# Ten raw buffers during expert 0, and a first gather in full single precision

## What is computed

```
def swiglu(h, w_gu, w_down):
    gu = h @ w_gu
    return (jax.nn.silu(gu[..., :FF_DIM]) * gu[..., FF_DIM:]) @ w_down

def moe_swiglu(h, w_router, w_gu, w_down):
    logits = (h @ w_router).astype(jnp.float32)
    top_vals, top_idx = lax.top_k(logits, TOP_K)
    gates = jax.nn.softmax(top_vals, axis=-1)
    comb = jnp.sum(jax.nn.one_hot(top_idx, N_EXPERTS, dtype=jnp.float32) * gates[..., None],
                   axis=-2).astype(h.dtype)
    y = jnp.zeros_like(h)
    for e in range(N_EXPERTS):
        y = y + comb[..., e:e + 1] * swiglu(h, w_gu[e], w_down[e])
    return y
```

## Time and profile before

| | us |
|---|---|
| runs | 1605.94, 1602.95, 1606.61 |
| median | 1605.94 |
| the profiled execution, its own time | 1605.62 |
| span of the profiled execution | 1603.5 |
| TensorE busy in it | 1525.8 (95%) |
| VectorE busy | 1244.3 (78%) |
| ScalarE busy | 1017.5 (63%) |
| GpSimd busy | 144.9 (9%) |
| DMA, mean rate | 284 GB/s |

### The profile page before, as it was taken

How to read it: one execution, slowest core, us unless ns; L and a number is a source line. 1 busy time by engine, 2 the same in 40 slices (tenths; PEclk the granted TensorE clock), 3 DMA queues, 4 the chain that set the end, 5 groups by cost and what they waited for, 6 DMA issues and landing times.

```text
span 1603.5 us, 21400 instructions
## 1 busy us (share of the span) xinstructions
PE 1525.8 (95%) x7237; PEld 1252.7 (78%) x7238; DVE 1244.3 (78%) x1094; ACT 1017.5 (63%) x922; POOL 144.9 (9%) x111
## 2 busy tenths in 40 slices
PE   8999999999989988889999999999999999999997
PEld 6888777888879866667887887788788878887875
DVE  6744655544459978898888989898989898889898
ACT  5344444344345756687776777777777777787785
POOL 0000000000000002803102202000130022000000
PEclk9999999999999989999999999999999999999999
DMA  9653455555553035999998999999999999999994
GB/s 343 228 188 129 150 191 184 184 183 186 197 169 106 27 132 173 396 397 364 396 383 313 384 375 331 365 356 375 340 389 359 370 343 388 357 371 340 372 369 176
DMA packets 197770, 456.10 MB, mean 284 GB/s; under 512 B 9076, under 2 KB 17852, under 8 KB 197695
## 3 DMA queue, kind: packets, MB, share of 16 engines
q1 hardware_dynamic: 193340, 444.84, 76.6%
q0 software_dynamic: 1728, 5.27, 0.9%
q10 hardware_dynamic: 2626, 4.93, 0.9%
HBM read 452.90 MB, written 2.11 MB: 284 GB/s over the span
## 4 chain that ended last, share of the span: by engine, by line
PE 75%; DVE 13%; DMA 4%; issue 4%; ACT 4%; DVEq 0%; ACTq 0%; POOL 0%; POOLq 0%; SPq 0%
PE bank L1869 17%; PE bank L1862 11%; PE bank L1863 11%; PE bank L1951 6%; DVE wlo L1095 5%; PE bank L1860 5%; PE bank L1940 4%; DMA raw<-in_moe_w_gu 4%; DVE y L1366 4%; PE bank L2104 3%; ACT whi L591 3%; PE bank L1892 3%; PE bank L1899 2%; PE bank L1893 2%; PE bank L1942 2%
## 5 line engine op out<-in xcount | busy, mean ns | idle before, releaser
L1095 DVE TENSOR_TENSOR wlo<-raw,whi 128x2048 fp32r<-128x2048 f32 x422 | 957.0, 2290 | 256.0 <-ACT whi L591 254.4
L591 ACT ACTIVATE whi<-raw 128x2048 fp32r<-128x2048 f32 x422 | 800.5, 1918 | 405.3 <-PE bank L1869 260.6
L1869 PE MATMUL bank<-wlo,xx 128*128 128x512 f32 x1200 | 328.6, 396 | 23.0 <-DVE wlo L1095 22.1
L1869 PEld LDWEIGHTS bank<-wlo,xx 128*128 128x128 f32 x1200 | 222.6, 189 | 86.3 <-DVE wlo L1095 41.6
L1862 PE MATMUL bank<-whi,xx 128*128 128x512 f32 x640 | 251.8, 393 | 1.5 <-DVE xx L1121 0.6
L1863 PE MATMUL bank<-whi,xx 128*128 128x512 f32 x640 | 249.7, 390 | 0.0
L1860 PE MATMUL bank<-whi,xx 128*128 128x512 f32 x560 | 157.3, 403 | 5.8 <-ACT whi L591 5.8
L1862 PEld LDWEIGHTS bank<-whi,xx 128*128 128x128 f32 x640 | 120.6, 188 | 27.2 <-issue 1.0
L1863 PEld LDWEIGHTS bank<-whi,xx 128*128 128x128 f32 x640 | 120.6, 188 | 24.5
L1860 PEld LDWEIGHTS bank<-whi,xx 128*128 128x128 f32 x560 | 104.3, 190 | 32.9 <-issue 12.0
L1951 PE MATMUL bank<-wlo,hT 128*128 128x512 f32 x392 | 107.5, 396 | 1.2 <-DVE wlo L1095 1.2
(11 more groups left out here) (326 smaller groups left out, 1818.0 us busy)
## 6 DMA issues: line engine op xcount, KB each, us to landing
raw<-in_moe_w_gu SPq DMA_DIRECT2D x224, 1024.0 KB, 7.5
raw<-in_moe_w_down SPq DMA_DIRECT2D x112, 1024.0 KB, 7.9
raw<-in_ffn_w_gu SPq DMA_DIRECT2D x28, 1024.0 KB, 5.0
raw<-in_ret_w_in SPq DMA_DIRECT2D x24, 1024.0 KB, 7.5
raw<-in_ffn_w_down SPq DMA_DIRECT2D x14, 1024.0 KB, 4.9
raw<-in_ret_w_out SPq DMA_DIRECT2D x8, 1024.0 KB, 4.9
raw<-in_conv_w_pw SPq DMA_DIRECT2D x16, 512.0 KB, 4.5
raw<-in_conv_w_pw SPq DMA_DIRECT2D x4, 1024.0 KB, 5.3
```

Source lines behind the costliest of these rows:

```text
L591: nc.scalar.activation(whi[base % SPLIT][:, :], raw[base % RAW][:, :], ACT.Copy).then_inc(hi_done, 1)
L1095: nc.vector.tensor_tensor(wlo[base % SPLIT][:, :], raw[base % RAW][:, :], whi[base % SPLIT][:, :].bitcast(f32), ALU.subtract).then_inc(lo_ ...
L1869: last = nc.tensor.matmul(dst[:, :], both, wl, start=False, stop=kc == DC - 1)
```

## The change

Expert 0's blocks use a ring of ten buffers: the six of `raw` and four `spare` ones that lie in the region behind `conv_at`, where `yh`, `sq`, `yl` and `hT32` are. `home` gives the buffer of a block. Blocks 0 to 5 lie in `raw`, 6 to 9 in the spares, 10 to 35 go round the ten, and 36 to 41 are in `raw` again, so that experts 1 and on find the ring of six. Of the first round, block 6 waits for the counter `lnb_ps` (end of the convolution's norm), block 8 for lo of block 0, block 9 for `lgT_ps` (router products done); from block 10 each waits for the block that had its buffer before.

Since the buffer of a block now is not a plain function of a loop variable, expert 0's steps are written out on SP, ScalarE and VectorE, in all variants of need, and the loop over e starts at 1 there. TensorE's loops stay. The `If(e > 0)` of ScalarE and VectorE become a choice at build time.

The gather of expert 0 multiplies z, scaled in place by ScalarE, with `onehot`, both as plain float32: 16 products, in place of 32 with fp32r operands and of the two that clear. `zh` and `zl` are gone, and so are VectorE's two instructions for `zl`. The copy of z to `z_rows` is issued before the gather's results are read. The side expert's two fetches go to place 2, behind its `build_onehot`, since their buffers are those of a spare; the side expert's own `build_onehot` stays at place 1.

```diff
+        spare = [at("spare0", [P, BLK], f32, m_at), at("spare1", [P, BLK], f32, conv_at + 8192),
+                 at("spare2", [P, BLK], f32, m_at + 8192), at("spare3", [P, BLK], f32, conv_at + 16384)]
+        ring = raw + spare
...
+        FIRST_RING = [(B_MOE + i) % RAW for i in range(RAW)] + [RAW + i for i in range(len(spare))]
+
+        def home(block, six=0):
+            turn_of = block - B_MOE
+            if not isinstance(six, int) or not 0 <= turn_of < MOE_BLOCKS:
+                return block % RAW
+            return FIRST_RING[turn_of % (len(ring) if turn_of < MOE_BLOCKS - RAW else MOE_BLOCKS - RAW)]
...
             def load(base, src, six=0):
-
-                if base >= RAW:
-                    sp.wait_ge(lo_done, base - RAW + 1 + 6 * six)
-                dst = raw[base % RAW][:, :].rearrange("p (c n) -> p c n", c=src.shape[1])
-                sp.dma_start(dst, src).then_inc(arrived[base % RAW], 16)
+                base, six = absolute(base, six)
+                place = home(base, six)
+                before = user_before(base) if isinstance(six, int) and base < B_MOE + MOE_BLOCKS else base - RAW
+                if before >= 0:
+                    sp.wait_ge(lo_done, before + 1 + 6 * six)
+                elif place == RAW:
+                    sp.wait_ge(lnb_ps, 1)
+                elif place == RAW + 2:
+                    sp.wait_ge(lo_done, B_MOE + 1)
+                elif place == RAW + 3:
+                    sp.wait_ge(lgT_ps, TILES)
+                dst = ring[place][:, :].rearrange("p (c n) -> p c n", c=src.shape[1])
+                sp.dma_start(dst, src).then_inc(landed_in[place], 16)
...
-                if place == 1:
+                if place == 2:
                     for t in range(2):
                         fetch(2 + t, SIDE, t).then_inc(side_rows_in, 16)
+                if place == 1:
                     build_onehot(side_onehot, SIDE).then_inc(side_onehot_done, 1)
...
-                nc.scalar.activation(zh[:, t, :], z[:, t, :], ACT.Copy, scale=rstd[:, t:t + 1]).then_inc(zh_done, 1)
-            nc.scalar.activation(identr[:, :], ident, ACT.Copy).then_inc(zh_done, 1)
+                nc.scalar.activation(z[:, t, :], z[:, t, :], ACT.Copy, scale=rstd[:, t:t + 1]).then_inc(zn_done, 1)
             hi(B_MOE + 2)
+            nc.scalar.activation(identr[:, :], ident, ACT.Copy).then_inc(identr_done, 1)
             act.wait_ge(lg_max, 1)
             nc.scalar.activation(rk[:, 0, :, :], rk[:, 7, :, :], ACT.Exp).then_inc(ex_done, 1)
             nc.scalar.activation(warm[:, 0:1], smallT[:, 0:1], ACT.Silu)
+            act.wait_ge(zn_done, 2)
+            for t in range(TILES):
+                act.dma_start(z_rows[t * P:(t + 1) * P, :], z[:, t, :]).then_inc(z_stored, 16)
...
-                with dve.Fori(0, STEPS - 1) as i:
+
+                def step(i):
                     lo(B_MOE + 6, six + i)
                     hidT_lo(done + 1 + i)
                     lo(B_MOE + 7, six + i)
...
+                if later:
+                    with dve.Fori(0, STEPS - 1) as i:
+                        step(i)
+                else:
+                    for i in range(STEPS - 1):
+                        step(i)
...
                     for t in range(TILES):
-                        where = rows_of[:, t, tile * P:(tile + 1) * P]
-                        nc.tensor.matmul(dst, zh[:, t, c * P:(c + 1) * P], where, start=t == 0, stop=False)
-                        last = nc.tensor.matmul(dst, zl[:, t, c * P:(c + 1) * P], where, start=False, stop=t == TILES - 1)
+                        last = nc.tensor.matmul(dst, z[:, t, c * P:(c + 1) * P],
+                                                onehot[:, t, tile * P:(tile + 1) * P].bitcast(f32),
+                                                start=t == 0, stop=t == TILES - 1)
...
-            pe.wait_ge(zh_done, 3)
-            first_gather()
+            pe.wait_ge(zn_done, TILES)
+            pe.wait_ge(onehot0_done, 1)
+            gather(0, gather_ps).then_inc(gather_ps, 1)
+            pe.wait_ge(identr_done, 1)
```

129 lines of the change are left out of this document (76 added, 53 removed).

## The result

| | us |
|---|---|
| before, five runs beside the changed kernel | 1606.29 median (1602.95 to 1606.61) |
| changed kernel, five runs | 1595.50 median (1595.16 to 1598.05) |
| ratio | 0.9946, 95% interval 0.9934 to 0.9958 |
| profiled execution of the changed kernel | 1595.50, span 1593.7 |
| forecast | 1593.4 (1589.6 to 1597.5) |

The change gains 10.8 us, against 12.2 (the sum) forecast. A second series gave 1598.32 against 1605.38 (ratio 0.9958, 0.9944 to 0.9972): there it gains 7.1. So the size was missed by 1.4 to 5.1 us, and it was missed where the prediction had put a 5% rival. The first series lies inside of the stated range, the second 0.8 us above it. One of the twelve executions of a later run, unroll_few, took 3072.88 us; no trace shows why, and it is in none of the medians and ratios given here.

The account below looks back on a forecast made before the run. Expert 0 was taken as bound by DMA, later experts by TensorE's pace. Ring 11.0, gather 0.9 and branches 0.3 give 12.2; 1605.6 - 12.2 = 1593.4 us, range 1589.6 to 1597.5.

Parts of the forecast that it names:

- the sum: Whole kernel: 11.0 us from the ring, 0.9 from the gather, 0.3 from loops and branches, 12.2 gained.
- 5% rival: VectorE or ScalarE leaving written-out expert 0: one instruction wait of 5 to 11.4 us, 1598.6 to 1604.6; 5%.
- both ledgers: Expert 0: gain by loads (DMA) 14.5 us, by the engines' pace 11.0; the smaller counts.
- a stall that stands beside a low clock: VectorE's first two steps from block 5 in expert 0: kept at 14.8 and 15.4 us, against 14.1 each later.

Follow-up runs that it names:

- unroll_few: Kernel before with expert 0's steps written out, ring of six, old gather, and no jumps over the other variants; 1605.53 us, ratio 1.0005.
- few_last_b: Repeat of the complete changed kernel with expert 0's variant for need 0 standing last on ScalarE and VectorE; 1591.18 us, ratio 0.9927.

## What to carry to other kernels

A change that needs written-out code can pay for the code that is jumped over, as ScalarE did here and VectorE did not: put the variant that runs last, so that the jump falls on its entry, if the engine waits there anyway, and look for a gap with the releaser "issue" behind each long branch. A buffer more is worth one block's transfer as long as loads bind, and nothing once the next engine does, so count both ledgers. In one trace a stall that stands beside a low clock may be chance: before it is kept in a sum, it should be seen twice.

## What the runs showed of the chip

- ScalarE's jump over 124 rows of written-out code took 5.4 us from the branch to the next instruction at a DMA share of 1.05 (5.07 to 5.15 us idle, five traces). A jump over the two variants at the entry took 2.5 to 2.8 us (at a share of 0.29 in few_last_b; 1.54 idle). One over 54 rows took 0.43 (0.14 idle). VectorE's jumps over 123 and 193 rows left no idle time where 1.9 us would be hidden; at the entry it took 0.5 us.
- The granted clock of TensorE falls to the lower level at the same few places. In all eighteen traces it does near 560, in seventeen near 620; near 464, 605, 720, 993 and 1549 it falls in some executions and not in others, also of the same kernel. Each fall comes behind short idle stretches of TensorE, the longest of them 0.9 to 4.3 us. One fall costs 1.2 us at the last two places.
- A product of 128 columns in full float32 takes two records of 0.12 us at full clock: 16 products in 3.81 us, against 4.39 for 32 products with fp32r operands and the wait of 0.4 between them. So the gain of that gather is mostly the wait.
